# A tenth place in the ring of gather buffers, from row 10 to row 29

## What is computed

```python
q = (hf @ w_q).reshape(T, 8, 2, 128)                 # 8 heads, two half queries each
s = einsum('thpd,hpnd->thpn', q, sub_keys)           # scores against 128 keys per half
sv, si = top_k(s, 16)                                # 16 best of each half
cv, ci = top_k(all 256 sums of a pair of halves, 16) # 16 experts of 16384 per head
g = softmax(cv)
u, v = u_tab[expert], v_tab[expert]                  # rows of 1024 numbers each
out = sum over experts of g * gelu(x . u) * v
```

## Time and profile before

| what | value |
|---|---|
| median of 3 runs | 1154.97 us (1154.26 to 1155.44) |
| the profiled execution's own time | 1154.77 us |
| its span, first to last instruction | 1153.0 us |
| mean granted PE clock | 0.975 |
| PE busy | 1033.9 us (90%) |
| DVE busy | 804.4 us (70%) |
| ACT busy | 549.0 us (48%) |
| POOL busy | 299.9 us (26%) |
| DMA, mean over the span | 338 GB/s |

### The profile page before, as it was taken

One profiled execution on the slowest core, in us unless ns is written; L12 is line 12 of the kernel. 1 busy time (PEld: TensorE's weight loads), 2 busy tenths in 40 slices (PEclk: granted clock), 3 DMA queues, 4 the chain that ended last, 5 costly groups with the idle time before them and its releaser, 6 DMA issues.

```text
span 1153.0 us, 13442 instructions
## 1 busy us (share of the span) xinstructions
PE 1033.9 (90%) x4830; PEld 675.9 (59%) x4830; DVE 804.4 (70%) x1680; ACT 549.0 (48%) x1303; POOL 299.9 (26%) x262
## 2 busy tenths in 40 slices
PE   6999999999999987886768888788799999999997
PEld 3798987644344333432323433333299978999986
DVE  6787886777676776878877655545476878887843
ACT  3465733433334332336876742222455666565631
POOL 0000002545345533455454454454000000000000
PEclk9999999999999998998998898899999999999999
DMA  9988697999999999999999999999875344545440
GB/s 378 423 354 323 249 387 288 397 422 421 422 421 420 422 421 422 420 422 422 422 422 420 422 422 421 421 422 422 360 333 202 129 182 167 195 188 188 178 146 37
DMA packets 48338, 390.08 MB, mean 338 GB/s; under 512 B 5514, under 2 KB 6034, under 8 KB 7316
## 3 DMA queue, kind: packets, MB, share of 16 engines
q0 software_dynamic: 37040, 269.51, 56.4%
q1 hardware_dynamic: 11236, 119.77, 26.4%
HBM read 388.20 MB, written 1.06 MB: 338 GB/s over the span
## 4 chain that ended last, share of the span: by engine, by line
PE 56%; DMA 32%; DVE 6%; ACT 5%; issue 2%; POOL 0%; SPq 0%; DVEq 0%; ACTq 0%
DMA ring<-in_uv,idx 29%; PE ps L1703 17%; PE ps L2135 10%; PE ps L2116 7%; PE ps L2295 5%; PE ps L1728 2%; PE ps L1884 2%; PE ps L1991 2%; PE ps L2223 2%; DMA ring<-in_w_ada 1%; DMA ring<-in_w_in 1%; DVE ring L1493 1%; DVE ring L1032 1%; ACT prob L882 1%; PE ps L1783 1%
## 5 line engine op out<-in xcount | busy, mean ns | idle before, releaser
L571 POOL DMA_INDIRECT ring<-in_uv,idx x247 | 287.9, 1166 | 317.8 <-PE ps L2135 149.8
L2116 PE MATMUL ps<-ring,probT 128*128 128x512 f32 x480 | 233.0, 642 | 59.7 <-ACT probT L888 59.7
L2135 PE MATMUL ps<-ring,probT 128*128 128x512 f32 x508 | 238.8, 606 | 32.1 <-ACT probT L888 32.1
L1493 DVE CUSTOM_DVE_ANT_0 ring<-h2t,ring 128x1024 f32<-128x1024 f32 x127 | 154.4, 1221 | 89.8 <-DMA ring<-in_uv,idx 89.4
L2116 PEld LDWEIGHTS ps<-ring,probT 128*128 128x128 f32 x480 | 95.3, 204 | 196.8 <-issue 109.9
L1703 PE MATMUL ps<-util_r,ring_r 128*128 128x256 f32 x1120 | 192.8, 282 | 0.3 <-ACT util L601 0.3
L2135 PEld LDWEIGHTS ps<-ring,probT 128*128 128x128 f32 x508 | 92.6, 192 | 154.6 <-issue 93.5
L1021 DVE TENSOR_TENSOR ring_r<-ring,ring_r 128x1024 fp32r<-128x1024 f32 (+1 forms) x134 | 155.5, 1203 | 35.1 <-ACT ring_r L597 35.1
L878 ACT ACTIVATE prob<-prob 128x2 f32<-128x2 f32 (+2 forms) x98 | 20.0, 204 | 316.4 <-DVE prob L1493 206.3
L1703 PEld LDWEIGHTS ps<-util_r,ring_r 128*128 128x128 f32 x1120 | 158.1, 188 | 1.3 <-issue 0.7
L597 ACT ACTIVATE ring_r<-ring 128x1024 fp32r<-128x1024 f32 (+1 forms) x134 | 132.0, 1039 | 38.0 <-PE ps L2295 19.1
(11 more groups left out here) (301 smaller groups left out, 1184.6 us busy)
## 6 DMA issues: line engine op xcount, KB each, us to landing
ring<-in_w_in SPq DMA_DIRECT2D x11, 2048.0 KB, 13.9
ring<-in_w_up SPq DMA_DIRECT2D x11, 2048.0 KB, 7.9
ring<-in_w_ada SPq DMA_DIRECT2D x7, 2048.0 KB, 9.2
ring<-in_w_down SPq DMA_DIRECT2D x6, 2048.0 KB, 7.9
ring<-in_w_ada SPq DMA_DIRECT2D x8, 1024.0 KB, 14.1
ring<-in_w_out SPq DMA_DIRECT2D x4, 2048.0 KB, 9.3
ring<-in_w_q SPq DMA_DIRECT2D x3, 2048.0 KB, 12.6
ring<-in_w_in SPq DMA_DIRECT2D x4, 1024.0 KB, 10.0
```

The source lines that it names most:

```text
L571: e.indirect_dma_start(out=row_buf[n], out_offset=None, in_=uv, in_offset=bass.IndirectOffsetOnAxis(ap=idx[:, tt, k:k + 1], axis=0)).then_inc(
L1493: e.tensor_tensor_reduce(u, h2t[:, tt, :], u, 1.0, 0.0, ALU.mult, ALU.add, av[:, tt, at:at + 1]).then_inc(*made.put(("dot", n)))
L2116: ins = e.matmul(acc[half][:, :], diag[:, (first + j) % DIAGS, :], row_buf[first + j][:, D + half * 512:D + (half + 1) * 512], start=False ...
L2135: ins = e.matmul(acc[half][:, :], diag[:, n % DIAGS, :], row_buf[n][:, D + half * 512:D + (half + 1) * 512], start=(k == 0), stop=(k == 127))
```

## The change

Three things change. (1) QUERIES_BUF joins the queue of places: it stands at the end of the first round, behind (3, 1), with row 0 as its former row, and it may be used up to row 30. (2) For the first tile, the queries of heads 2 and 3 are written to the blocks of heads 0 and 1, whose scores are done by then (`query_place`); ACT waits for those scores. (3) The copies of the later pairs of heads wait for the last row in QUERIES_BUF.

```diff
-LAST_ROW_OF = {VALUES_BUF: 44, MERGED_BUF: 24}
+LAST_ROW_OF = {VALUES_BUF: 44, MERGED_BUF: 24, QUERIES_BUF: 30}
...
-    queue, had, out = deque(FIRST_BUFS), {}, [(QUERIES_BUF, None)]
+    queue, had, out = deque((*FIRST_BUFS, QUERIES_BUF)), {QUERIES_BUF: 0}, [(QUERIES_BUF, None)]
...
+def query_place(h, tt):
+
+    return 2 * (h - EARLY_HEADS) if tt == 0 and EARLY_HEADS <= h < 2 * EARLY_HEADS else 2 * h
...
                 if h >= EARLY_HEADS:
-                    act.wait_ge(done, ("rows", LEFT_AT[VALUES_BUF] if h >= 6 else 0))
-                e.activation(Q3[:, 2 * h:2 * h + 2, tile[tt]],
+                    act.wait_ge(done, ("scores", h - EARLY_HEADS, tt))
+                j = query_place(h, tt)
+                e.activation(Q3[:, j:j + 2, tile[tt]],
...
-                if c == 3:
-                    act.wait_ge(done, ("rows", LEFT_AT[VALUES_BUF]))
+                act.wait_ge(done, ("rows", LEFT_AT[VALUES_BUF if c == 3 else QUERIES_BUF]))
...
-                    ins = e.matmul(o[:, z * P:(z + 1) * P], Q3[:, 2 * h + z, tile[tt]], keys3[:, 2 * h + z, :], start=True,
+                    ins = e.matmul(o[:, z * P:(z + 1) * P], Q3[:, query_place(h, tt) + z, tile[tt]], keys3[:, 2 * h + z, :], start=True,
```

## The result

The changed kernel takes 1161.3 us (median of 4 runs, 1160.99 to 1162.69), the kernel before 1154.81 us (median of 4 runs beside it). The ratio is 1.0055, 95% interval 1.0043 to 1.0067: slower by 5.0 to 7.7 us. The forecast was 1159.2 us, in a range of 1157.0 to 1161.2 us. The direction was right; the middle was 2.1 us too low, and the median lies 0.1 us above the end of the range. The profiled execution took 1161.35 us with a span of 1159.5 us, against 1154.77 and 1153.0 us, so the two traces differ by 6.5 us of span, and that is what has to be found in them. (In the changed kernel the lines of the code are numbered 5 higher: L2135 is L2140, L2183 is L2188.)

What follows compares the result with a forecast made beforehand. The prediction took the DMA byte stream to bound the gather, and PE behind the last row. It summed -1.2 us (head) and +5.6 us (later load) to +4.4 us on 1154.77: 1159.2 us, range 1157.0 to 1161.2 us.

Steps and rivals of the forecast that it cites:

- What bounds the gather: Gather of the 256 rows: the stream of bytes is the bound, DMA share 1.01 at about 421 GB/s.
- Rival (d): Gather: the ring sets the rows' pace, so more places gain 7.3 us; 1153.1 us; chance 0.05 with its variant.
- Part 1: Dip at 210 to 218 us: rows 10 and later issue one row earlier, gaining 1.2 us (0 to 1.8).
- Rival (a): Head of the gather: the earlier issues gain nothing, as the slowest engine wasn't dry; 1160.4 us; chance 0.13.
- Part 2: Rows 47 to 51 have seven places, not eight: 0 us, at worst giving back part 1's 1.2 us.
- Part 3: First-tile queries: same instructions and sizes, nothing waits for the new places: 0 us.
- Part 4: Start of the second block: its first load, in2 2, waits for row 255 and issues 6.72 us later: +5.6 us.
- Its lower bound: Second block's first load: on empty engines the half lands in 3.7 us, so the seam costs 4.4 us.
- rival (b): Seam cheaper, landing in 3.7 us on empty engines, with the full 1.8 us gained at the head: 1157.4 us; chance 0.11.
- Rival (c): Second block: in2 0 or in2 1 comes late, the full 6.7 us pass on, no head gain: 1161.5 us; chance 0.08.
- and then the same groups of PE with the same gaps, shifted: Expected sign of part 4: behind PE's wait of some 7 us for ACT, its second-block work is only shifted.

Runs made afterwards that it cites:

- ten profiles: One profile each of the kernel before, the changed kernel and eight follow-up kernels; PE's gather ended at mean 834.20 us without the tenth place, 833.42 with.
- the ladder: Three runs on the kernel before, SP's first in2 2 load waiting for row 253, 254 or 255 instead of 249: 1156.83, 1159.57 and 1162.42 us.
- the kernel in which PE was kept busy: Changed kernel plus 30 unused identity matmuls on PE between the last row and the second block: 1159.53 us, ratio 1.0039.
- the wait for row 254: Kernel before, with SP waiting for PE to be done with row 254, not 249, before issuing in2 2: 1159.57 us, ratio 1.0043.
- the queries alone: Changed kernel with the nine places of before, keeping only the new columns for the first-tile queries of heads 2 and 3: 1154.98 us, ratio 1.0002.
- the wait for row 255: Kernel before, with SP waiting for PE to be done with row 255, not 249, before issuing in2 2: 1162.42 us, ratio 1.0062.
- the turned slots: Changed kernel with the second block's weight chunks in other slots, so row 255 isn't in slot 3, where in2 2 was: 1153.92 us, ratio 0.9993.
- the place for row 10: Changed kernel with QUERIES_BUF usable up to row 11 instead of 30, so it has rows 0 and 10 only: 1154.22 us, ratio 0.9991.
- the waits for rows 255 and 253: Kernel before, with SP waiting for row 255 or 253, not 249, before issuing in2 2: 1162.42 us and 1156.83 us.

## Why the prediction was right, and where it was short

**What bounds the gather: right.** Share 1.01 and 420 to 422 GB/s stand in both traces, however many places are in use. Rival (d), that the ring sets the pace, had 1153.1 us and is out: the tenth place gave 0.8 us, not 7.3.

**Part 1, rows 10 and later: right in mechanism, somewhat too large.** Row 10 went out at 207.11 us (206.8 expected), 1.4 us earlier. The working had the next rows 1.7 us or a little more earlier as well; row 11 came only 0.93 us earlier. Rows 11 and 13 now wait for nothing but POOL's own issue of the row ahead, which takes 1.88 and 1.98 us for the two rows in `area` that are now rows 10 and 12 (1.81 us for the one in the earlier trace rows); the prediction left out that term. The rate in the dip rose by 55 GB/s in the profile after, and by 42 in the means of ten, not by the whole 93. Forecast 1.2 us, measured 0.8 over ten profiles and 1.0 in the profile after. Rival (a), no gain, is out by the ten profiles.

**Part 2, seven places for rows 47 to 51: right.** Share 1.01 and 420 GB/s at 312 to 332 us.

**Part 3, the queries: right.** 1154.98 against 1155.15 us.

**Part 4, the later load: right to 0.1 us.** Issue behind PE's last row, landing after 4.9 us, split of 2.0 us, standstill of 7.14 us: +5.62 us where the forecast had +5.6. Its lower bound, and with it rival (b), took the 4.9 us for a time with other transfers in the way. They weren't: on empty engines (DMA share 0.00 at 832 to 834 us in the trace after) it is 4.9 us again, and so it is on the three steps of the ladder, within 0.2 us. The Trainium skill's 2.0 us plus bytes, page "DMA: Bandwidth & Descriptors", section "Anatomy of one DMA — SWDGE (gpsimd) path", gives 4.4 us by its figures, an estimate; the measured 4.9 to 5.1 us decide. That section and the page's table of measured sizes with its 6.15 us for 1 MB are both for DMAs that POOL issues, and this one is SP's, which the prediction overlooked.

**Rival (c), a later load sets the pace: out,** though its 1161.5 us is the nearest number to the result. In2 1 is late for ACT (1.76 us of waiting, 1.33 before), but PE doesn't wait for it: the distance to the kernel before is 5.78 us ahead of PE's use of it (863.83 against 858.05 us) and still 5.79 us at 962.59 us, far behind it. A rival may have the right number by a wrong road; the standstill at the start of the block shows which it was.

**The step that failed** is the sentence "and then the same groups of PE with the same gaps, shifted". The groups and gaps are the same, but not their durations: PE's clock falls in or just behind the longer standstill, and the first 3 to 5 us of work run at half of it. That is +1.16 us in the profile after, 1.3 us by the kernel in which PE was kept busy, 2.2 us in one run. The prediction never asked what a standstill of 7 us would do to the granted clock, though the trace of before could have priced it: the earlier trace rows have a clock of 0.96 and 0.95 over the gather. In that trace PE stands still for 5.40 us at about 530 us, and works behind it at half clock (the windows 534 to 536 and 536 to 538 us have 0.50). There the stream of bytes hides the loss; at the seam nothing does. The timeline of PE, before:

```profile
535.76 8.92 PE L2116 MATMUL ps<-ring,probT 128*128 128x512 f32 x16 [5.40 <-ACT probT L888]
545.19 7.13 PE L2116 MATMUL ps<-ring,probT 128*128 128x512 f32 x16 [0.50 <-ACT probT L888]
```

Sixteen such matmuls take 8.92 us behind the long standstill and 7.13 us at full clock, so that fall took 1.8 us of PE's time. With the measured terms the sum is -0.8 + 5.6 + 1.2 = +6.0 us, 1160.8 us.

**The rest is not the change's.** The second fall, 0.7 us in the profile after, stands in three of ten profiled executions: after, the wait for row 254, and the queries alone. It is missing in the other seven, the kernel before and the one with the wait for row 255 among them. The standstill there is 2.05 us in all that were read. Whether the changed kernel falls there more often than the one before isn't known: of an execution without a profile only the mean clock over the span is on record, and in the kernel before that mean alone spreads from 0.971 to 0.982. The +6.0 us lie within the interval of the ratio (5.0 to 7.7 us) without it.

## What to carry to other kernels

A ring that gets one more place also changes which place the last item has, and a load that waits for "the last user of its slot" may move by a whole stage; read the table's last rows before its first ones, and turn the slots so that the first load of the next stage finds the place that was left earliest (here that alone was worth some 7 us, 1161.3 against 1153.9 us). When you lengthen a standstill of PE, price not only the standstill but the half clock behind it. And this ring was long enough wherever the DMA share was 1.01, with seven places as with twelve: look for the few microseconds in which the share is lower, and try the added place for those rows alone.

## What the runs showed of the hardware

- **PE's clock at the seam.** Ahead of it PE is busy for 1.98 us of every 2.46 us, at clock 1.00. After a standstill of 1.51 or 1.52 us (before, the turned slots, the queries alone, the place for row 10) it stayed at 1.00. After 2.46, 4.59, 7.09 and 7.14 us it fell to 0.50 (one profiled execution each), and the 16 matmuls took 3.35 to 3.75 us instead of 2.12. At 2.46 us it fell only when PE was at work again. With PE filled up to a gap of 0.70 us it stayed. Elsewhere, a standstill of 2.05 us had a fall in three of ten executions. And within the gather, behind 16 matmuls of rows, all ten have a standstill of 2.8 us at about 512 us: the clock fell there in four of them (after, the waits for rows 255 and 253, the queries alone) and stayed in six, the kernel before among them; after the 5.40 us at about 530 us it fell in all ten. So between 2.0 and 2.8 us it is open, and it differs from execution to execution at the same place; what decides it wasn't settled.
- **The price of a fall isn't fixed:** at the seam 1.16 us twice, 1.21 us after the shortest standstill, 2.2 us once after 7.09 us, where 7.14 us had cost 1.16; at the second place 0.7, 0.8 and 1.0 us. The Trainium skill, page "TensorE: Matmul & The Clock Gate", section "Part 1: The HAM clock gate (the "warmup" mystery)", says that the number of matmuls at the low clock varies between runs of one kernel, and that in the three kernels measured there the clock had two levels alone. The traces agree: windows of 2 us have 1.00 and 0.50, and values between them only where it changes.
- **The first 1 MB of the next stage's weights,** with the second half issued 0.4 us behind it, landed 4.8 to 5.2 us after SP's issue in the ten profiled executions: 4.9 us with the engines still bringing the last row (before), and 4.9 us with DMA share 0.00 ahead of it (after).
- **A float32 matmul of 128 x 128 by 128 columns** stands twice in the trace and takes 0.23 us for both at full clock.
